# Sparse attention: value products for four blocks every second cycle, a ring of six transposed blocks, and the compressed part loaded per unit

## The reference

```python
p_sel = masked_softmax(s - sl * dist, (tok <= t[:, None])[:, :, None])
o_sel = jnp.einsum('bghql,bgqld->bqghd', p_sel.astype(dt), vg)
...
p_win = masked_softmax(s - sl * d_i.astype(jnp.float32), valid)
o_win = jnp.einsum('bghqk,bkgd->bqghd', p_win.astype(dt), vwc)
return gc[..., 0:1] * o_cmp + gc[..., 1:2] * o_sel + gc[..., 2:3] * o_win
```

## Time and profile before

| | us |
|---|---|
| median of 3 runs | 3420.95 (3409.36 to 3424.22) |
| profiled execution, its own time | 3418.37 |
| its span | 3416.6 |
| sparse attention in it | 1225 to 1995.9 |
| TensorE busy over the span | 2990.3 |
| VectorE, ScalarE, GpSimd busy | 1345.3, 1000.7, 558.6 |

### The profile page before, as it was taken

One profiled execution on the slowest core, in us unless ns is written; L12 is line 12 of the kernel. 1 busy time (PEld: TensorE's weight loads), 2 busy tenths in 40 slices (PEclk: granted clock), 3 DMA queues, 4 the chain that ended last, 5 costly groups with the idle time before them and its releaser, 6 DMA issues. The chain is left out here.

```text
span 3416.6 us, 37491 instructions
## 1 busy us (share of the span) xinstructions
PE 2990.3 (88%) x13210; PEld 1767.3 (52%) x13211; DVE 1345.3 (39%) x3149; ACT 1000.7 (29%) x2050; POOL 558.6 (16%) x568
## 2 busy tenths in 40 slices
PE   8999999999977758989999969999699899859990
PEld 5644444444446635555665646666544355547670
DVE  3421212111114545555565647777511111152236
ACT  1100000000005524545555536666411012113332
POOL 0121110111003330221222120000121100001116
PEclk9999999999988769999999979999899999969995
DMA  3211211121141220011111020110254333615848
GB/s 118 77 63 68 71 66 57 68 71 65 59 143 47 80 84 27 15 51 35 55 41 49 7 93 1 38 38 1 111 219 144 143 129 123 270 60 208 319 166 307
DMA packets 120754, 323.41 MB, mean 95 GB/s; under 512 B 13216, under 2 KB 49696, under 8 KB 112416
## 3 DMA queue, kind: packets, MB, share of 16 engines
q1 hardware_dynamic: 100320, 247.54, 20.5%
q0 software_dynamic: 14096, 51.39, 4.6%
q10 hardware_dynamic: 6192, 22.55, 1.6%
HBM read 206.42 MB, written 115.02 MB: 94 GB/s over the span
## 5 line engine op out<-in xcount | busy, mean ns | idle before, releaser
L305 PE MATMUL p_ps<-token_sums,p_ws 128*128 128x512 f32 x768 | 340.0, 592 | 0.0
L305 PEld LDWEIGHTS p_ps<-token_sums,p_ws 128*128 128x128 f32 x768 | 145.9, 190 | 183.8 <-issue 183.8
L305 PE MATMUL p_ps<-xnT,p_w 128*128 128x512 f32 x512 | 233.1, 598 | 5.2 <-PEq L59 5.2
L1683 PE MATMUL o_ps<-o_w,o_mT 128*128 128x512 f32 x512 | 224.2, 596 | 14.0 <-DMA o_w<-in_w_out 14.0
L314 ACT ACTIVATE p_kept<-p_ps 128x512 f32<-128x512 f32 x32 | 19.1, 598 | 737.4 <-PE p_ps L305 737.4
L1038 PE MATMUL b_po<-b_probT,vsw 128*64 128x256 f32 (+1 forms) x1824 | 231.1, 375 | 0.0
L1113 DVE CUSTOM_DVE_ANT_0 b_prob_s<-b_pq,b_sel 128x896 f32<-128x896 f32 (+5 forms) x192 | 167.8, 911 | 144.0 <-PE b_pq L997 124.4
L327 DVE TENSOR_TENSOR p_kept<-p_ps,p_kept 128x512 f32<-128x512 f32 x96 | 66.4, 692 | 391.6 <-PE p_ps L305 391.6
L1275 PE MATMUL d_pq<-d_keys,d_q 64*128 64x512 f32 (+3 forms) x640 | 177.7, 589 | 27.4 <-DVE d_seg_max L1381 15.1
L1381 DVE CUSTOM_DVE_ANT_0 d_prob<-d_pq,d_bias 128x1024 f32<-128x1024 f32 (+6 forms) x192 | 167.5, 910 | 72.7 <-PE d_pq L1275 70.2
L997 PE MATMUL b_pq<-ks,b_q 64*128 64x512 f32 (+3 forms) x688 | 166.0, 542 | 29.0 <-DVE b_seg_max L1113 16.1
(11 more groups left out here) (277 smaller groups left out, 4755.9 us busy)
## 6 DMA issues: line engine op xcount, KB each, us to landing
projT<-p_stage SPq DMA_DIRECT2D x128, 256.0 KB, 2.3
y<-e_y ACTq DMA_DIRECT2D x43, 512.0 KB, 4.3
p_w<-in_wt SPq DMA_DIRECT2D x16, 1024.0 KB, 5.5
gates_T<-projT SPq DMA_DIRECT2D x16, 1024.0 KB, 9.9
wgu<-in_w_gu SPq DMA_DIRECT2D x4, 4096.0 KB, 15.7
y<-m_zeros POOLq DMA_DIRECT2D x20, 512.0 KB, 11.8
p_xin<-in_x SPq DMA_DIRECT2D x16, 512.0 KB, 3.7
mergedT<-m_stage SPq DMA_DIRECT2D x8, 1024.0 KB, 11.4
```

The source lines that it names most:

```text
L305: mm = nc.tensor.matmul(ps[n % 8][:], weights[:, k, :], moving[:, k, :], start=(k == 0), stop=(k == HK - 1))
L1683: mm = nc.tensor.matmul(ps[b][k][:], mT[:, b, dt, :], w[:, dt, k * 512:(k + 1) * 512], start=(dt == 0), stop=(dt == DT - 1))
```

## The change

The value products are made in even cycles only, each time for the four blocks of the two cycles before. The ring `probT` grows from four to six blocks, and the copies into it wait for the block six back. The loops run longer by up to two cycles, and a unit's `output` stands three cycles after its last instead of two. `ya` is no longer loaded for a whole pair (both tiles, 512 columns) after the pair's distances, but for each unit (both tiles, 128 columns), two units ahead.

```diff
@@ -847,17 +847,17 @@
...
-    final = cycles + 2
+    final = cycles + 3
...
-        ya = [sb(f"ya{b}", [P, 2, NSA_HEADS * HD]) for b in range(2)]
+        ya = [sb(f"ya{b}", [P, 2, P]) for b in range(2)]
...
-        probT = sb("probT", [P, 4, 512])
+        probT = sb("probT", [P, 6, 512])
...
@@ -904,9 +904,12 @@
...
-                if k >= 2:
-                    sp.wait_ge(turned, end[last_unit[k - 2]])
-                sp.dma_start(ya[b][:], d["ya"][:, 2 * p:2 * p + 2, :]).then_inc(ya_in[b], 16)
+
+            def load_compressed(u):
+                p, i = units[u]
+                if u >= 2:
+                    sp.wait_ge(turned, end[u - 2])
+                sp.dma_start(ya[u % 2][:], d["ya"][:, 2 * p:2 * p + 2, i * P:(i + 1) * P]).then_inc(ya_in[u % 2], 16)
...
@@ -917,7 +920,11 @@
...
             load(0)
             load(1)
+            load_compressed(0)
+            load_compressed(1)
             for u in range(NU):
+                if u + 2 < NU:
+                    load_compressed(u + 2)
                 store(u)
...
@@ -1013,10 +1020,9 @@
...
                 elif kind == "C":
-                    if i == 0:
-                        pe.wait_ge(ya_in[(u // PAIRS) % 2], 16 * (u // PAIRS // 2 + 1))
+                    pe.wait_ge(ya_in[u % 2], 16 * (u // 2 + 1))
...
@@ -1036,21 +1042,22 @@
...
-                                          probT[:, f % 4, g * w:(g + 1) * w],
+                                          probT[:, f % 6, g * w:(g + 1) * w],
...
-            for c in range(-2, cycles + 1):
+            for c in range(-2, cycles + 3):
...
-                for f in (2 * c - 2, 2 * c - 1):
-                    if 0 <= f < NF and flats[f][1] in "SW":
-                        values(f)
+                if c % 2 == 0:
+                    for f in range(2 * c - 4, 2 * c):
+                        if 0 <= f < NF and flats[f][1] in "SW":
+                            values(f)
...
@@ -1076,10 +1083,10 @@
...
-                    reuse = [x for x in blocks if x % 4 == f % 4 and x < f]
+                    reuse = [x for x in blocks if x % 6 == f % 6 and x < f]
...
@@ -1148,7 +1155,7 @@
...
-                    if (end[u] - 1) // 2 + 2 == c:
+                    if (end[u] - 1) // 2 + 3 == c:
                         output(u)
```

More of the change, by code:

```diff
@@ L1015, in turn @@
                 elif kind == "C":
-                    if i == 0:
-                        pe.wait_ge(ya_in[(u // PAIRS) % 2], 16 * (u // PAIRS // 2 + 1))
+                    pe.wait_ge(ya_in[u % 2], 16 * (u // 2 + 1))
                     for j in range(2):
-                        mm = nc.tensor.transpose(pt[f % 2][:, j * P:(j + 1) * P], ya[(u // PAIRS) % 2][:, j, i * P:(i + 1) * P], s.ident[:])
+                        mm = nc.tensor.transpose(pt[f % 2][:, j * P:(j + 1) * P], ya[u % 2][:, j, :], s.ident[:])
                 else:
@@ L1078, in copy @@
                     w = GROUPS * len(tiles) * P
-                    reuse = [x for x in blocks if x % 4 == f % 4 and x < f]
+                    reuse = [x for x in blocks if x % 6 == f % 6 and x < f]
                     if reuse:
                         act.wait_ge(used, used_after[reuse[-1]])
-                    nc.scalar.activation(probT[:, f % 4, 0:w], pt[f % 2][:, 0:w], ACT.Copy).then_inc(act_copied, 1)
+                    nc.scalar.activation(probT[:, f % 6, 0:w], pt[f % 2][:, 0:w], ACT.Copy).then_inc(act_copied, 1)
             for c in range(-2, final):
@@ L1132, in copy @@
                 dve.wait_ge(turned, f + 1)
-                reuse = [x for x in blocks if x % 4 == f % 4 and x < f]
+                reuse = [x for x in blocks if x % 6 == f % 6 and x < f]
                 if reuse:
                     dve.wait_ge(used, used_after[reuse[-1]])
-                nc.vector.tensor_copy(probT[:, f % 4, 0:w], pt[f % 2][:, 0:w]).then_inc(dve_copied, 1)
+                nc.vector.tensor_copy(probT[:, f % 6, 0:w], pt[f % 2][:, 0:w]).then_inc(dve_copied, 1)
             def output(u):
```

## The result

| | before | changed |
|---|---|---|
| median of 4 runs, us | 3420.78 (3409.36 to 3424.22) | 3459.15 (3454.66 to 3468.07) |
| profiled execution: own time, span | 3418.37, 3416.6 | 3459.57, 3457.8 |
| sparse attention in it | 1225 to 1995.9 | 1225 to 2043.1 |

The changed kernel is slower: the ratio of the times is 1.0114, with a 95% interval of 1.0100 to 1.0128. That is 38 us, where the prediction had 20.

The account below looks back on a forecast made before the run. TensorE was taken to set the pace, through its work with gaps between kinds and its waits. Terms 9 + 12.8 + 5.1 + 7.2 - 1.7 - 7.2 - 4.8 = +20.4 us on 3418.4 gave 3439, stated as 3441; range 3418 to 3463.

Parts of the forecast that it names:

- the late copies of VectorE: Six cycles without scores where VectorE's scaling delays its copies: value products move behind the wait, 0.85 each, +5.1 us.
- the longer V: Value products of four blocks in even cycles cover waits of scores for VectorE at 15 places: -7.2 us.
- ordinary pairs: 30 odd cycles without scores, copies prompt: the second transposes wait for a copy, 0.3 each, +9 us.
- output product: VectorE's product of output and scales, a cycle later, no longer delays copies at 8 places, 0.6 each: -4.8 us.
- pairs with scales and compressed part: Odd cycles without scores, with scales and compressed part: short value products move into a gap, 0 us.
- Behind exponentials: 15 cycles without scores, ScalarE's copy behind exponentials: value products done after the wait, 0.85 each, +12.8 us.
- Too early scores: 16 odd cycles with scores before even ones with scores: scores wait for VectorE, 0.62 less 0.17 each, +7.2 us.
- ring and load: Six-block ring and compressed part loaded per unit: both at no cost, covered by TensorE's order and early loads.
- Faster: Rival: copies don't hold the second transposes of a pair; only borders and longer value products count, -43 us, 3378; chance 0.10.
- No change: Rival: waits for exponentials partly shrink and gains are more frequent; half the losses, +3 us, 3424; chance 0.24.
- More waits than counted: Rival: all 60 cycles with scores lose 0.45, and half clock follows three to five waits; +50 us, 3471; chance 0.10.
- Transposes and the clock: Rival: runs of 16 transposes bring TensorE's clock down to 1.2 GHz, 51 us more; chance 0.03.

Follow-up runs that it names:

- e1: Changed kernel with value products back in every cycle, two blocks each; ring, load per unit and later output kept: 3415.34 us, ratio 0.9984 to the kernel before.
- e5: Changed kernel, but value products left out only in odd cycles with scores: 3420.84 us, ratio 0.9999 to the kernel before.
- e6: Changed kernel, but value products left out only in odd cycles without scores: 3447.88 us, ratio 1.0083 to the kernel before.
- e2: Changed kernel with four extra unused products in each of 14 odd cycles whose copies stand behind exponentials: 3450.28 us, ratio 1.0089 to the kernel before.

## Why the prediction was right, and where it fell short

The direction was right, and 3459 lies in the range of 3418 to 3463, but near its upper end, 18 us above 3441. Most terms held in mechanism. The clock and the scores were priced far too low, and two terms, the late copies of VectorE and the longer V, are hardly found in the time. I compared the two timelines pair by pair: the time of an odd cycle and the even one behind it, after less before, from T to T. These sums are worked out from some 260 cycles, and add up to the stage's growth (28.6 + 3.0 + 3.7 + 11.5 = 46.8).

**Borders and ordinary pairs.** Forecast was 2.47 us for two T where copies are prompt, the second T 1.35 after the first. The changed kernel, all engines:

```profile
1350.97 0.86 PEld L1031 LDWEIGHTS b_pt<-ident,b_prob_s 128*128 128x128 f32 x8 [0.38 <-issue]
...
1351.67 1.29 DVE L1143 COPY b_probT<-b_pt 128x512 f32<-128x512 f32 x2 [0.17 <-PE b_pt L1031]
...
1352.41 0.42 PEld L1031 LDWEIGHTS b_pt<-ident,b_prob_s 128*128 128x128 f32 x4 [0.58 <-DVE b_probT L1143]
...
1353.01 0.42 PEld L1031 LDWEIGHTS b_pt<-ident,b_prob_s 128*128 128x128 f32 x4 [0.18 <-DVE b_probT L1143]
...
1353.60 0.30 PEld L1004 LDWEIGHTS b_pq<-ks,b_q 64*128 64x128 f32 x4 [0.17 <-issue]
```

The second T stands 1.44 after the first, and the two take 2.63: the mechanism, with the copy 0.70 behind T's start as in the earlier trace rows. The 40 pairs of this kind, the six behind VectorE's scaling among them, gave +3.0 us together, where +9, +5.1 and part of the -4.8 for the output product were forecast, some +10. The +5.1 is the term that wasn't there. V was taken to lie wholly in the waits for VectorE's late scaling, at 0.85 each. Against e1, where the output product is out of the way too, these six pairs are -0.12 to +0.40 us longer, 1.0 in all: their second T starts at 1.44 to 1.86 behind the first, where e1 has 1.91 to 2.64. The 8 pairs with scales and compressed part, put at 0, gave +3.7.

**Behind exponentials.** This is where most of the miss lies. The 15 places were right. Forecast was 0.85 each, 12.8. Six of them show 0.86 to 1.18, mean 0.97: the mechanism and nearly the size. The other nine show 2.13 to 3.38, mean 2.53, and each has a stretch at half clock in it. Together the 15 cost 28.6 us. The longer the wait, the more often the clock fell: behind the five waits of 2.5 to 3.0 us each time, behind the four of 2.11 three times, behind the six of 1.3 to 1.7 once. That the difference is the clock can be seen in three units of pair 3 that do the same work:

```profile
1851.80:1874.90 23.10, 20.04 (x146) 12.24 (x144) 13.25 (x29) 11.88 (x26) 2.59 (x4) 1.00 0.05 13
1874.90:1899.70 24.80, 21.74 (x147) 12.99 (x145) 13.25 (x29) 11.99 (x27) 2.59 (x4) 0.93 0.40 133
1899.70:1922.80 23.10, 20.05 (x146) 12.25 (x144) 13.25 (x29) 11.88 (x26) 14.93 (x12) 1.00 0.05 13
```

The middle one has 3.4 us at half clock and is 1.7 longer, of which 1.6 by T to T. The same place in it and in the next unit:

```profile
1889.98 0.42 PEld L1031 LDWEIGHTS b_pt<-ident,b_prob_w 128*128 128x128 f32 x4 [0.93 <-DVE b_probT L1143]
...
1892.25 0.42 PEld L1031 LDWEIGHTS b_pt<-ident,b_prob_w 128*128 128x128 f32 x4 [1.26 <-ACT b_probT L1089]
1892.87 0.51 PEld L1004 LDWEIGHTS b_pq<-kw,b_q 64*128 64x128 f32 x4 [0.20 <-issue]
```

```profile
1914.72 0.42 PEld L1031 LDWEIGHTS b_pt<-ident,b_prob_w 128*128 128x128 f32 x4 [0.93 <-DVE b_probT L1143]
...
1916.99 0.42 PEld L1031 LDWEIGHTS b_pt<-ident,b_prob_w 128*128 128x128 f32 x4 [1.26 <-ACT b_probT L1089]
1917.58 0.30 PEld L1004 LDWEIGHTS b_pq<-kw,b_q 64*128 64x128 f32 x4 [0.17 <-issue]
```

Equal waits, and then a group of loads that takes 0.51 in the one and 0.30 in the other.

The slow unit of pair 3 is also the one with the DMA traffic (0.40), which would be another cause. Pair 5 rules it out. The same place in three of its units, where the pairs last 7.22, 5.59 and 7.23 us:

```profile
1752.80:1760.10 7.30, 5.38 (x29) 3.11 (x29) 1.71 (x3) 3.50 (x6) 0.00 (x0) 0.77 0.01 2
1784.30:1790.00 5.70, 3.79 (x29) 2.39 (x30) 1.70 (x3) 3.50 (x6) 0.00 (x0) 1.00 0.08 28
1814.20:1821.50 7.30, 5.43 (x29) 3.08 (x30) 1.66 (x3) 3.46 (x6) 0.76 (x1) 0.77 0.01 2
```

The two slow ones have less DMA than the fast one, and 3.4 us at half clock each, for 1.6 us.

The step that fell short most is the size of the clock's term. The prediction knew it only as part of a rival ("three to five such places with some 5 us at 1.2 GHz are 10 us") and left it out of the sum, which priced these places with "V is now done behind it, at its full 0.85". Measured: 58.0 - 17.1 = 40.9 us more at half clock, by 1.6 / 3.4 = 0.47 each, is 19 us. The sum of 20.4 with it is 39.6; the median moved by 38.4. The agreement is partly luck: the stage grew by 47.2, so it holds 28 us without the clock, 8 more than the sum, and the stages behind gave 6 back. The 8 are what is left of larger misses, which in part cancel: the scores and the pairs with compressed part came out dearer than forecast, the ordinary pairs cheaper.

**Scores.** "Waits of scores about as long as before" was wrong as a total (51.0 for 40.3), though both its parts were there. Too early scores waited 15.7 us more in e5, where 16 x 0.62 = 10 was forecast; the longer V took 6.2 us of waits away in e6, where 7.2 was forecast. In the table of pairs, odd cycles with scores give +11.5, where +7.2 - 1.7 - 7.2 = -1.7 was forecast: +17.7 where the next cycle has scores too, -6.2 where it has none. This is the second term that was mis-sized. The prediction counted 16 odd cycles with V due and scores both in them and behind them, at 0.45; by the kernel's lists there are 30, and their pairs gave 0.6 each. And little of the 7.2 is in the time. At the place of the earlier trace rows the scores no longer wait, and the odd cycle is 1.83 us shorter (2.72 for 4.55), but the next T now waits for VectorE's copies (the 0.82 at 1322.82 above), and the pair gains 0.32.

**Output product, ring, load.** The 4.8 for the output product are the 4.9 of e1, and ring and load are free in its trace, as forecast. The loads in the changed kernel take 2.6 us to landing, between the stores' 1.9 and the old loads' 10.0 of the earlier trace rows, and no wait for them is in the list:

```profile
b_ya<-ya_compressed SPq DMA_DIRECT2D x32, 128.0 KB, 2.6
```

**What was to be seen.** T T at 2.4 to 2.7 us: yes. V of 16 at 1.88: yes at full clock (1.87 in e2). Waits of transposes "from 63 to about 95": 92.7. The stage "to about 791": 818, the clock and 8 us more.

**The rivals.** "Faster" wanted the copies to let the second T start within 1.2 us of the first; in prompt pairs of 8 transposes it starts at 1.34 to 1.44. "No change" had the exponentials' places halved; they doubled. "More waits than counted" had the right cause and too little of it: nine places with half clock instead of three to five, 19 us instead of 10. Its other half, 0.45 lost in each of the 44 cycles with scores, was not found: of the 60 with scores and V, the 30 with no scores behind them gave -4.3 together. "Transposes and the clock" is refuted. The Trainium skill, page "TensorE: Matmul & The Clock Gate", Part 4, says that transposes don't bring the full clock; here the window 1316 to 1326 has three groups of T (1316.76, 1319.48, 1322.82) and the clock at 1.00, as have the 23 us from 1340 to 1363 around the run of 16 at 1350.97. At the nine places it fell at waits. The same page ("Why this matters for your kernels") asks to keep TensorE free of long idle gaps between bursts, or it falls back to half clock. The place at 1326 agrees, with its wait of 2.96. At 1892 no single gap was longer than 1.26, with two groups of four transposes between, and the clock still fell, while behind the same gaps a unit later it did not. A look at single gaps doesn't settle it there, and no run here shows what does.

## What to carry to other kernels

A piece of work that stands inside a wait is free here, and it also keeps TensorE's clock up (e2); moving it behind the wait costs its own length (0.97 us for 0.85 of work here) and, where the clock falls, as much again and more (2.53). Before grouping work to save borders of 0.17 us, look at what each separated piece was covering, and price every wait that grows twice: once for its length, once for the half clock behind it. When a wait of the kernel hangs on one engine's long instruction, try to move the few short jobs behind it to another engine before you reorder the engine that waits: 20 copies gave 12 us here, and with the output product moved 22 to 27, where this reordering alone lost 44.

## What the runs showed of the hardware

- More work on TensorE made a kernel faster: 56 extra products with unused results, 8.9 us less.
- A stretch of 3.4 us at half clock cost 1.6 us. It began between 0.7 us before the end of the wait (1326.13, wait over at 1326.80) and 1.5 behind it, and lay on the work that the wait had held back. Of 15 waits of one kind nine were followed by one, all five of 2.5 us and more, and of the same gaps in two units of pair 3 (0.93 and 1.26 us) one was and the other wasn't. From such rows a clock term can be forecast only as a share of places.
